# Two transformer-like blocks on one core: the first products after each norm start with high parts, in free PSUM banks

## The chip, the cores and the metric

The kernel runs on one core of one Trainium2 chip. The metric is device time in microseconds (us), the median of three runs. PE is the matmul engine, PEld its weight loads, DVE the vector engine, ACT the scalar engine, POOL the GpSimd engine, and SP the engine that issues nearly all DMAs. Each has its own instruction queue and executes it in order; they meet at semaphores.

## The reference

A sequence of 256 rows of width 1024 (batch 1) passes three layers, all in float32. Each layer is a chain of stages of the same form: normalise the rows, multiply by weights, add to the residual.

```python
# layers 1 and 2; the mixer is attention in the first, an S5 state-space model with GLU in the second
x = x + 0.5 * rmsnorm(swiglu(rmsnorm(x, g[0]), w_in, w_out), g[1])
h = rmsnorm(x, g[2]); x = x + rmsnorm(mixer(h), g[3])
x = x + 0.5 * rmsnorm(swiglu(rmsnorm(x, g[4]), w_in2, w_out2), g[5])
gate = sigmoid(rmsnorm(x, g[6]) @ w_gate)
x = x + rmsnorm(gate * (p[i] @ w_proj), g[7])
# layer 3: as above without the second norm; its mixer is a 128-wide window attention
# beside a gated linear recurrence; rmsnorm at the very end
swiglu(h, w_in, w_out) = (silu(h @ w_in[:, :2816]) * (h @ w_in[:, 2816:])) @ w_out
```

## The kernel before, in words

**Products in two parts.** Every float32 operand is split into a high part (rounded to the matmul format) and a low part (the rest). A product is three matmuls: high by high, high by low, low by high. For the weights, ACT writes the high part (`whi`, L627) from the raw tile that a DMA brought, and DVE the low part (`wlo`, L1103). For the normed rows, PE transposes them into PSUM (L1885), ACT writes `xhi` (L687) from there, and DVE `xlo` (L1208).

**Weights as a ring.** The weights are a stream of 528 half-units of 128x1024. `raw` holds two pairs of half-units, `whi` and `wlo` hold four half-units. A slot of the ring is written again only when PE has reported the half-unit in it as used (`s_used`), and a slot of `raw` is loaded again only when DVE has made the low part of both half-units in it (`s_lo`). At the start of a stage two or all four of its first half-units are ready; where two, ACT splits the next two behind what the change of stage asks of it.

**Settling.** Between two stages the 256 rows are settled in two halves h = 0, 1 of 128 rows: squares (ACT), the reciprocal root (POOL), the residual and the norm (DVE), eight transposes (PE, `transposed`), `xhi` in two quarters kq = 0, 1 (ACT, `evict_hi`), `xlo` in two quarters (DVE, `evict_lo`). `take_turns` writes out the order of these steps over the halves; hooks hang other work behind a step. There are 13 settlings, k = 0 to 12. While it waits, PE runs matmuls on a weight tile whose result nobody reads (`meanwhile`, `fill_in`).

**Stages behind a settling.**
- `ffn(n)`, n = 0 to 5, behind k = 0, 2, 4, 6, 8, 10. Its first half-unit is 24 matmuls of 128x256 (`half_unit`), with both halves of the rows as columns. Column f of the product goes to PSUM bank 4 + f % 3.
- `attention`, behind k = 1: its values product (`values("v0", ...)`) takes four half-units for h = 0 and then for h = 1; the settling of h = 1 (its transposes) comes in between, behind the second half-unit.
- `mixers`, behind k = 9: half-units as in `ffn`, in banks 4 and 5.
- `ple(layer)`, behind k = 3, 7, 11: `project`, a small product of another input, goes to banks 4 to 7 during the settling, and ACT keeps its result in SBUF (`keep`, L741), behind step 7 of the settling. Then comes the gate product into the same banks: `linear` with a head of four half-units through `run`, with the transposes of h = 1 in the middle of it as in `values`.
- The S5 stage and the last store are no part of the change.

**What the first product waits for.** PE waits for `s_xlo` of the whole half or of both halves, that is for the last low part of the rows. In `ffn` bank 4 is also one that the transposes of h = 0 wrote.

Of the kernel before, what the change touches and what calls it, by code (L numbers as in the profile page):

```python
# [8 lines left out]
S = 256  # L9
# [50 lines left out]
SCORE_AT = [j + 2 for j in QK_AT]  # L60

# [65 lines left out]
def program(nc, w, rows, cols, pT, b1c, ssm_s, ssm_b, ssm_c, ssm_cc, oh, idn, eo, x, out, scr):  # L127
# [4 lines left out]
    with ctx:  # L132
# [141 lines left out]
        lv, lp = hf[:, 0, :], hf[:, 1, 0:128]  # L274
# [129 lines left out]
        def sync(sp):  # L404
# [213 lines left out]
        def scalar(a):  # L618
# [79 lines left out]
            def ffn(n):  # L698
                def up(f):
# [8 lines left out]
                    b = 4 + f % 3  # L708
# [20 lines left out]
            def ple(layer):  # L729
# [4 lines left out]

                def keep():
# [11 lines left out]
                settle(k, {3: project, 7: keep})  # L747
# [165 lines left out]
            def mixers():  # L913
# [89 lines left out]
                for j in range(2):  # L1003
                    q.wait_ge(s_used, pair())
                    a.activation(fq[:, 2 * j:2 * j + 2, :], two(4 + n % 2), ACT.Sigmoid).then_inc(m_sf, 1)
# [87 lines left out]
        def vector(v):  # L1093
# [122 lines left out]
            def ffn(n):  # L1216
                def up(f):
# [6 lines left out]
                    v.tensor_tensor(hf[:, f % 2, :], PS[:, 4 + f % 3, S:2 * S], sg[:, f % 2, :], MUL).then_inc(s_hm, 1)  # L1224
# [556 lines left out]
        def tensor(pe):  # L1781
# [13 lines left out]
            def run(parts, base, last, by_half=None, finish=None, step=2, between=None):  # L1795

                for h in range(2):
                    if by_half is not None:
                        q.wait_ge(s_xlo, n_ev(by_half, h))
                    if between and h:  # L1800
                        between()
                    for n, (u, ahi, alo, first, end) in enumerate(parts):
                        if finish and h == 0 and n == 2:
                            finish()
                        hi, lo = weight(u)
                        l_hi, l_lo = ahi[:, 128 * h:128 * h + 128], alo[:, 128 * h:128 * h + 128]
                        for i, (l, r) in enumerate(((l_hi, hi), (l_hi, lo), (l_lo, hi))):
                            for c in range(2):
                                e = mm(PS[:, base + step * h + c, :], l, r[:, 512 * c:512 * c + 512], first and i == 0, end and i == 2)
                        if h:  # L1810
                            e.then_inc(s_used, 1)
                        elif last and n == len(parts) - 1:
                            e.then_inc(s_y, 1)

            def linear(name, acts, base=0, head=1, tail=1, by_half=None, finish=None, ready=None, n_fill=1, step=2, between=None, after=None):
                kts = len(acts)
                v0 = LAST[name] - kts + 1
                for ks in groups(kts, head, tail):
# [8 lines left out]
                    run(parts, base, ks[-1] == kts - 1, by_half if first else None, finish if first else None, step, None if ks[0] else between)  # L1827
                    bg.fill(n_fill)
# [3 lines left out]
            def half_unit(u, o):  # L1832
                hi, lo = (a.rearrange("p (k n) -> p k n", k=8) for a in weight(u))
                for k in range(8):
                    mm(o, hi[:, k, :], xhi[:, k, :], k == 0, False)
                    mm(o, hi[:, k, :], xlo[:, k, :], False, False)
                    e = mm(o, lo[:, k, :], xhi[:, k, :], False, k == 7)
                e.then_inc(s_used, 1)
# [59 lines left out]
            def ffn(n):  # L1898
                k = (0, 2, 4, 6, 8, 10)[n]

                def up(f):
                    b = 4 + f % 3
# [78 lines left out]
            def attention():  # L1981
                def values(name, cols, bank, ns, last, by_half=None):
# [3 lines left out]
                    for h in range(2):  # L1986
                        if by_half is not None:
                            q.wait_ge(s_xlo, n_ev(by_half, h))
                        for n in ns:
                            if by_half is not None and h == 0 and n == 2:  # L1990
# [3 lines left out]
                            for k in range(per):  # L1994
                                kt = per * n + k
                                l_hi, l_lo = (a[:, 128 * h:128 * h + 128] for a in x_acts[kt])
                                for i, (l, r) in enumerate(((l_hi, hi), (l_hi, lo), (l_lo, hi))):
                                    e = mm(PS[:, bank + h, cols], l, r[:, k, :], kt + i == 0, kt == 7 and i == 2)
# [107 lines left out]
            def mixers():  # L2106
# [11 lines left out]
                def pair():  # L2118
                    b = 4 + nb[0] % 2
                    bank_free(nb[0])  # L2120
                    nb[0] += 1
                    half_unit(u0[0], PS[:, b, 0:S])
# [129 lines left out]
                q.wait_ge(s_xlo, n_ev(9, 1))  # L2252
# [242 lines left out]
```

## Time and profile before

| | us |
|---|---|
| median of 3 runs | 1849.22 (1845.55 to 1850.02) |
| profiled execution | 1851.22 |
| its span | 1849.4 |
| PE busy | 1737.1 (94%) |
| DVE busy | 1098.5 (59%) |
| ACT busy | 881.5 (48%) |
| DMA, first queue | 298.66 MB, 45.3% of 16 engines |

The engines' busy shares say that PE is the engine to look at. The mean clock granted to it was 0.972 of full speed. The chain of waits says which engine held the end at each time; the timelines around the eleven stage starts say what PE waits for there.

### The profile page before, as it was taken

Reading aid. Unit: us, or ns where it says so; the run is one execution under the profiler, and the core shown is the slowest. Engines: PE = TensorE matmul, PEld = TensorE weight load, DVE = VectorE, ACT = ScalarE, POOL = GpSimd, SP = SyncE. Lnnn points to the kernel's source line nnn. Section 1 sums busy time; section 2 is a strip of 40 time slices with the busy share of each in tenths; the row PEclk is TensorE's granted clock in tenths of the full one; section 3 lists DMA queues with packets and bytes.
Section 4 is the critical chain, followed back from the end, with each engine's and each line's share of the span. In section 5 each row is a group of like instructions: output and inputs, shape, how many; then the busy total and the mean of one; then the engine's idle time right before and its main releaser. Section 6 shows DMA issues by size and latency. Waiting matters only on the chain.

```text
span 1849.4 us, 28076 instructions
## 1 busy us (share of the span) xinstructions
PE 1737.1 (94%) x11935; PEld 1593.0 (86%) x11935; DVE 1098.5 (59%) x1411; ACT 881.5 (48%) x1370; POOL 166.4 (9%) x192
## 2 busy tenths in 40 slices
PE   7999999899988999998989998999989997999996
PEld 6899789799977998977879997899979887799995
DVE  5455567578765444768565555655556575655554
ACT  5344466443555455452454445544444444444443
POOL 0000001218001012800000000000000000000000
PEclk9999999999999999998999999999999998999998
DMA  6755434445543443531445554465544332455551
GB/s 223 248 175 192 160 140 143 150 183 180 185 171 149 158 165 143 184 136 46 150 153 182 197 179 172 148 215 193 187 151 180 115 115 69 155 196 180 190 184 68
DMA packets 51084, 300.97 MB, mean 163 GB/s; under 512 B 6072, under 2 KB 12688, under 8 KB 17168
## 3 DMA queue, kind: packets, MB, share of 16 engines
q1 hardware_dynamic: 50800, 298.66, 45.3%
q8 instruction: 94, 1.54, 0.3%
q0 software_dynamic: 160, 0.52, 0.1%
q14 instruction: 30, 0.25, 0.0%
HBM read 298.08 MB, written 1.09 MB: 162 GB/s over the span
## 4 chain that ended last, share of the span: by engine, by line
PE 72%; DVE 11%; ACT 9%; DMA 4%; issue 3%; POOL 1%; SPq 0%; DVEq 0%; ACTq 0%; POOLq 0%
PE PS L1786 69%; DVE wlo L1103 4%; DMA raw<-in_w 3%; ACT whi L627 3%; ACT wk L670 1%; PE PS L1789 1%; POOL st L519 1%; PE PS L1885 1%; ACT SC L761 1%; DVE X L1180 1%; DVE SC L1341 1%; DVE xn L1188 1%; ACT SC L848 1%; DVE SC L1496 0%; DVE xlo L1208 0%
## 5 line engine op out<-in xcount | busy, mean ns | idle before, releaser
L1103 DVE TENSOR_TENSOR wlo<-raw,whi 128x1024 fp32r<-128x1024 f32 x528 | 664.5, 1267 | 435.9 <-ACT whi L627 434.3
L1786 PE MATMUL PS<-xhi,whi 128*128 128x256 f32 x2536 | 729.1, 287 | 17.7 <-DVE xlo L1208 9.8
L627 ACT ACTIVATE whi<-raw 128x1024 fp32r<-128x1024 f32 x528 | 550.6, 1054 | 396.1 <-PE PS L1786 230.0
L1786 PE MATMUL PS<-xlo,whi 128*128 128x256 f32 x2536 | 722.7, 285 | 0.0
L1786 PE MATMUL PS<-xhi,wlo 128*128 128x256 f32 x2536 | 722.5, 285 | 0.0
L1786 PEld LDWEIGHTS PS<-xhi,whi 128*128 128x128 f32 x2536 | 492.0, 194 | 26.5 <-DVE xlo L1208 11.4
L1786 PEld LDWEIGHTS PS<-xlo,whi 128*128 128x128 f32 x2536 | 492.3, 194 | 2.1
L1786 PEld LDWEIGHTS PS<-xhi,wlo 128*128 128x128 f32 x2536 | 491.7, 194 | 0.0
L1786 PE MATMUL PS<-whi,hhi 128*128 128x512 f32 x544 | 170.6, 395 | 2.4 <-DVE wlo L1103 2.4
L1786 PE MATMUL PS<-wlo,hhi 128*128 128x512 f32 x544 | 168.6, 391 | 0.0
L1786 PE MATMUL PS<-whi,hlo 128*128 128x512 f32 x544 | 168.3, 390 | 0.0
L709 ACT ACTIVATE wk<-PS 128x256 f32<-128x256 f32 x132 | 50.3, 381 | 156.8 <-PE PS L1786 156.6
L1786 PEld LDWEIGHTS PS<-wlo,hhi 128*128 128x128 f32 x544 | 102.6, 189 | 22.3
L1786 PEld LDWEIGHTS PS<-whi,hlo 128*128 128x128 f32 x544 | 102.4, 188 | 22.1
L1786 PEld LDWEIGHTS PS<-whi,hhi 128*128 128x128 f32 x544 | 98.0, 190 | 19.3 <-DVE wlo L1103 3.0
L1224 DVE TENSOR_TENSOR wk<-PS,wk 128x256 f32<-128x256 f32 x132 | 55.7, 422 | 91.5 <-ACT wk L709 91.3
L512 POOL TENSOR_SCALAR st<-st 128x1 f32<-128x1 f32 x36 | 11.7, 325 | 1072.4 <-ACT wk L670 551.2
L713 ACT ACTIVATE hhi<-wk 128x256 fp32r<-128x256 f32 x132 | 55.2, 418 | 111.0 <-DVE wk L1224 111.0
L1786 PE MATMUL PS<-whi,xhi 128*128 128x512 f32 (+2 forms) x272 | 89.2, 386 | 14.3 <-ACT SC L741 11.8
L1226 DVE TENSOR_TENSOR hlo<-wk,hhi 128x256 fp32r<-128x256 f32 x132 | 60.3, 457 | 63.9 <-ACT hhi L713 63.9
L1786 PE MATMUL PS<-wlo,xhi 128*128 128x512 f32 (+2 forms) x272 | 87.6, 380 | 0.0
L1786 PE MATMUL PS<-whi,xlo 128*128 128x512 f32 (+2 forms) x272 | 87.4, 379 | 0.0
(261 smaller groups left out, 1451.8 us busy)
## 6 DMA issues: line engine op xcount, KB each, us to landing
raw<-in_w SPq DMA_DIRECT2D x264, 1024.0 KB, 4.8
gr<-in_rows SPq DMA_DIRECT2D x23, 512.0 KB, 3.8
SC<-scratch SPq DMA_DIRECT2D x1, 2048.0 KB, 8.4
SC<-scratch SPq DMA_DIRECT2D x2, 1024.0 KB, 8.4
X<-in_x SPq DMA_DIRECT2D x2, 512.0 KB, 4.9
xn<-in_sc SPq DMA_DIRECT2D x2, 512.0 KB, 6.8
out<-xn SPq DMA_DIRECT2D x2, 512.0 KB, 2.7
SC<-in_pT SPq DMA_DIRECT2D x3, 256.0 KB, 4.2
```

Of the source, the lines that this page charges most:

```text
L519: g.tensor_tensor(r, ms, mh[:, 0:max(n, 1)], ALU.pow).then_inc(done, 1)
L627: a.activation(whi[:, u % NSPLIT, :], raw[:, u // 2 % NRAW, u % 2 * HU:u % 2 * HU + HU], ACT.Copy).then_inc(s_hi, 1)
L670: a.activation(wk[:, f], X[:, h, f], ACT.Square, scale=1 / 32, accum_out=ss[:, i:i + 1]).then_inc(s_sq, 1)
L709: a.activation(sg[:, f % 2, :], PS[:, b, 0:S], ACT.Silu).then_inc(s_silu, 1)
L713: a.activation(hhi[:, f % 4, :], hf[:, f % 2, :], ACT.Copy).then_inc(s_hhi, 1)
L761: e = a.activation(pr[:, m, l:z], sc[:, m, l:z], ACT.Exp, bias=n4[:, m, c:c + 1], accum_out=s4[:, m, c:c + 1])
L848: e = a.activation(cst[r, k, :, s, 16 * i:16 * i + 16], o[k][r], ACT.Copy)
L1103: v.tensor_tensor(wlo[:, u % NSPLIT, :], src, hi.bitcast(f32), SUB).then_inc(s_lo, 1)
L1180: v.scalar_tensor_tensor(X[:, h, f], src[:, f], by, X[:, h, f], MUL, ADD).then_inc(s_X, 1)
L1224: v.tensor_tensor(hf[:, f % 2, :], PS[:, 4 + f % 3, S:2 * S], sg[:, f % 2, :], MUL).then_inc(s_hm, 1)
L1226: v.tensor_tensor(hlo[:, f % 4, :], hf[:, f % 2, :], hhi[:, f % 4, :].bitcast(f32), SUB).then_inc(s_hlo, 1)
L1786: return pe.matmul(o, l, r, start=start, stop=stop)
```

## The change

Four edits, with the semaphores kept.

1. **High parts first.** `first_half_unit` takes the place of `half_unit` for the first half-unit of each `ffn` and of `mixers`: for each of eight row tiles it waits for that quarter's `xhi` alone and makes the two products with the high rows; then it waits for `xlo` and makes the eight products with the low rows. In `values("v0")` and in the head of the gate product (`run`), the same is done over the four half-units of each h: sixteen matmuls with high rows, then eight with low rows. `s_used` of a half-unit is counted with its low products.
2. **Other banks.** The first column of `ffn` goes to bank 3 in place of 4, and the first pair of `mixers` to bank 2.
3. **`keep` earlier.** ACT keeps the result of `project` right behind it (hook 3), not behind step 7.
4. **`lv`, `lp` elsewhere.** Two small attention vectors move from the shared `wk` to `prs[1]`, and SP loads them before settling 1, without waiting for the norm.

```diff
+def up_bank(f):
+    return 4 + f % 3 if f else 3
+def pair_bank(n):
+    return 4 + n % 2 if n else 2
...
+            sp.dma_start(lv, ssm_s[2].to_broadcast([128, 256])).then_inc(l_lam, 16)
             settle_rows(1)
-            weights(LAST["v0"])
-            q.wait_ge(s_xn, n_two(1, 1))
-            sp.dma_start(lv, ssm_s[2].to_broadcast([128, 256])).then_inc(l_lam, 16)
...
-                settle(k, {3: project, 7: keep})
+                settle(k, {3: project})
...
 (run)
                 for h in range(2):
-                    if by_half is not None:
-                        q.wait_ge(s_xlo, n_ev(by_half, h))
...
+                    if by_half is not None:
+                        q.wait_ge(s_xhi, n_ev(by_half, h, 0))
+                    for low in (False, True) if by_half is not None else (None,):
+                        if low:
+                            q.wait_ge(s_xlo, n_ev(by_half, h, 0))
...
+            def first_half_unit(u, o, settled):
+                hi, lo = (a.rearrange("p (k n) -> p k n", k=8) for a in weight(u))
+                for k in range(8):
+                    q.wait_ge(s_xhi, n_ev(settled, 1, k // 4))
+                    mm(o, hi[:, k, :], xhi[:, k, :], k == 0, False)
+                    mm(o, lo[:, k, :], xhi[:, k, :], False, False)
+                for k in range(8):
+                    q.wait_ge(s_xlo, n_ev(settled, 1, k // 4))
+                    e = mm(o, hi[:, k, :], xlo[:, k, :], False, k == 7)
+                e.then_inc(s_used, 1)
...
                     if f == 0:
-                        q.wait_ge(s_xlo, n_ev(k, 1))
-                    half_unit(up_at(n, f), PS[:, b, 0:S])
+                        first_half_unit(up_at(n, f), PS[:, b, 0:S], k)
```

On PE, the second gate product (k = 7) from its first matmul on, before. `whi` and `wlo` are its half-units' weights, `idt` rows the transposes of h = 1, and a wait for `s_lo` begins a half-unit:

```order
L1786 MATMUL PS<-whi,xhi 128x512 [waits s_lo,s_xlo,s_prj]
L1786 MATMUL PS<-whi,xhi 128x512
L1786 MATMUL PS<-wlo,xhi 128x512 x2
L1786 MATMUL PS<-whi,xlo 128x512 x2
L1786 MATMUL PS<-whi,xhi 128x512 [waits s_lo]
L1786 MATMUL PS<-whi,xhi 128x512
L1786 MATMUL PS<-wlo,xhi 128x512 x2
L1786 MATMUL PS<-whi,xlo 128x512 x2
L1885 MATMUL PS<-idt,xn 128x128 [waits s_xn]
```

The same stretch after:

```order
L1790 MATMUL PS<-whi,xhi 128x512 [waits s_lo,s_xhi,s_prj]
L1790 MATMUL PS<-whi,xhi 128x512
L1790 MATMUL PS<-wlo,xhi 128x512 x2
L1790 MATMUL PS<-whi,xhi 128x512 [waits s_lo]
L1790 MATMUL PS<-whi,xhi 128x512
L1790 MATMUL PS<-wlo,xhi 128x512 x2
L1910 MATMUL PS<-idt,xn 128x128 [waits s_xn]
```

The low products of the first two half-units no longer stand ahead of the transposes: eight matmuls stand there, not twelve. On PE, the end of the same head (its last two half-units for h = 1, up to the fifth half-unit, which waits for `s_lo`), before:

```order
L1786 MATMUL PS<-whi,xhi 128x512 x2
L1786 MATMUL PS<-wlo,xhi 128x512 x2
L1786 MATMUL PS<-whi,xlo 128x512 x2
L1786 MATMUL PS<-whi,xhi 128x512 x2
L1786 MATMUL PS<-wlo,xhi 128x512 x2
L1786 MATMUL PS<-whi,xlo 128x512 x2
L1786 MATMUL PS<-whi,xhi 128x512 [waits s_lo]
```

and after:

```order
L1790 MATMUL PS<-whi,xhi 128x512 x2
L1790 MATMUL PS<-wlo,xhi 128x512 x2
L1790 MATMUL PS<-whi,xlo 128x512 [waits s_xlo]
L1790 MATMUL PS<-whi,xlo 128x512 x7
L1790 MATMUL PS<-whi,xhi 128x512 [waits s_lo,s_xlo]
```

The eight low products stand at the end in one piece, and with them all four reports of a used half-unit. Before, these came with the 6th, 12th, 18th and 24th matmul of h = 1; now with the 18th, 20th, 22nd and 24th.

On ACT, the same settling, from the weight tile that precedes it, before (L687 writes `xhi`, L670 squares of h = 1, L741 is `keep`):

```order
L627 ACTIVATE whi<-raw 128x1024
L687 ACTIVATE xhi<-PS 128x4x128 [waits s_tr] x2
L670 ACTIVATE wk,st<-X 128x512 [waits s_sq,s_X] x2
L741 ACTIVATE SC<-PS 128x1024 [waits s_y]
L741 ACTIVATE SC<-PS 128x1024 [waits s_used]
```

and after (the lines are L693, L676, L745 there):

```order
L633 ACTIVATE whi<-raw 128x1024
L745 ACTIVATE SC<-PS 128x1024 [waits s_y]
L745 ACTIVATE SC<-PS 128x1024 [waits s_used]
L693 ACTIVATE xhi<-PS 128x4x128 [waits s_tr] x2
L676 ACTIVATE wk,st<-X 128x512 [waits s_sq,s_X] x2
```

The two copies of the projection stand ahead of the high parts and squares, whose order is kept.

## Rows read from the trace of the kernel before

**Rows 1.** Page, chain that ended last: share of the span by engine.
```profile
PE 72%; DVE 11%; ACT 9%; DMA 4%; issue 3%; POOL 1%; SPq 0%; DVEq 0%; ACTq 0%; POOLq 0%
```

**Rows 2.** Waits: engine and line, released by, us in total, times, longest us.
```profile
PE PS L1786 <- DVE xlo L1208: 12.2, 7, 2.5
PE PS L1786 <- ACT SC L741: 11.8, 3, 4.0
```

**Rows 3.** Chain in order of time: start us, us, what; stage starts and matmul rates.
```profile
944.23 184.32 PE PS L1786 x1308
...
1149.61 16.36 PE PS L1786 x72
...
1184.06 185.24 PE PS L1786 x1310
...
1381.30 54.29 PE PS L1786 x406
...
1532.71 2.88 PE PS L1786 x24
...
1608.24 1.98 PE PS L1885 x8
1611.62 194.85 PE PS L1786 x1348
```

**Rows 4.** Timeline, ACT at k = 6, 8, 9: start, us, what, [idle before].
```profile
941.92 1.21 ACT L687 ACTIVATE xhi<-PS 128x512 fp32r<-128x512 f32 x2 [1.65 <-PE PS L1885]
...
1182.08 1.08 ACT L687 ACTIVATE xhi<-PS 128x512 fp32r<-128x512 f32 x2 [2.56 <-PE PS L1885]
...
1378.93 1.26 ACT L687 ACTIVATE xhi<-PS 128x512 fp32r<-128x512 f32 x2 [1.58 <-PE PS L1885]
```

**Rows 5.** Timeline, DVE behind k = 6.
```profile
947.99 3.50 DVE L1103 TENSOR_TENSOR wlo<-raw,whi 128x1024 fp32r<-128x1024 f32 x3 [0.26 <-ACT whi L627]
```

**Rows 6.** Timeline, DVE and PE behind k = 2, DVE behind k = 4.
```profile
361.47 0.61 DVE L1345 TENSOR_SCALAR SC<-SC 128x32 f32<-128x32 f32 x3 [4.95 <-DMA SC<-in_par]
...
365.58 0.50 PE L1786 MATMUL PS<-xhi,whi 128*128 128x256 f32 x1 [1.91 <-DVE wlo L1103]
...
608.19 0.69 DVE L1345 TENSOR_SCALAR xn<-xn 128x1024 f32<-128x1024 f32 x1 [5.69 <-DMA xn<-in_sc]
```

**Rows 7.** Chain: heads of values (k = 1), second and third gate.
```profile
218.64 4.62 PE PS L1786 x12
...
1144.32 4.42 PE PS L1786 x12
...
1811.32 5.34 PE PS L1786 x12
```

**Rows 8.** Timeline, ACT and DVE at the second gate (k = 7).
```profile
1142.34 1.92 ACT L741 ACTIVATE SC<-PS 128x1024 f32<-128x1024 f32 x2
...
1145.24 2.36 DVE L1103 TENSOR_TENSOR wlo<-raw,whi 128x1024 fp32r<-128x1024 f32 x2 [0.33 <-ACT whi L627]
...
1153.82 1.06 ACT L627 ACTIVATE whi<-raw 128x1024 fp32r<-128x1024 f32 x1 [3.52 <-PE PS L1786]
...
1154.91 2.53 DVE L1103 TENSOR_TENSOR wlo<-raw,whi 128x1024 fp32r<-128x1024 f32 x2 [3.78 <-ACT whi L627]
...
1162.30 2.04 ACT L627 ACTIVATE whi<-raw 128x1024 fp32r<-128x1024 f32 x2 [3.41 <-DMA raw<-in_w]
...
1166.00 1.03 ACT L745 ACTIVATE xn<-PS 128x1024 f32<-128x1024 f32 x1 [0.35 <-PE PS L1786]
```

**Rows 9.** Timeline, ACT at the third gate (k = 11).
```profile
1833.94 1.03 ACT L745 ACTIVATE xn<-PS 128x1024 f32<-128x1024 f32 x1 [5.80 <-PE PS L1786]
```

**Rows 10.** Timeline, DVE at the values product (k = 1).
```profile
220.82 2.35 DVE L1103 TENSOR_TENSOR wlo<-raw,whi 128x1024 fp32r<-128x1024 f32 x2
```

**Rows 11.** Windows, PE: us, busy (instructions), granted clock, DMA share, GB/s.
```profile
216.00:218.00 2.00, 0.18 (x2) 1.00 0.50 172
218.00:220.00 2.00, 1.36 (x4) 0.73 0.01 4
```

More of the change, by code:

```diff
@@ L1004, in mixers @@
                     q.wait_ge(s_used, pair())
-                    a.activation(fq[:, 2 * j:2 * j + 2, :], two(4 + n % 2), ACT.Sigmoid).then_inc(m_sf, 1)
+                    a.activation(fq[:, 2 * j:2 * j + 2, :], two(pair_bank(n)), ACT.Sigmoid).then_inc(m_sf, 1)
                     n += 1
@@ L1797, in run @@
                 for h in range(2):
-                    if by_half is not None:
-                        q.wait_ge(s_xlo, n_ev(by_half, h))
                     if between and h:
                         between()
[L1802 to L1813, printed above, removed]
+                    if by_half is not None:
+                        q.wait_ge(s_xhi, n_ev(by_half, h, 0))
@@ new lines, in run @@
+                    for low in (False, True) if by_half is not None else (None,):
+                        if low:
+                            q.wait_ge(s_xlo, n_ev(by_half, h, 0))
+                        for n, (u, ahi, alo, first, end) in enumerate(parts):
+                            if finish and h == 0 and n == 2 and not low:
+                                finish()
+                            hi, lo = weight(u)
+                            l_hi, l_lo = ahi[:, 128 * h:128 * h + 128], alo[:, 128 * h:128 * h + 128]
+                            for i, (l, r) in enumerate(((l_hi, hi), (l_hi, lo), (l_lo, hi))):
+                                if low is None or low == (i == 2):
+                                    for c in range(2):
+                                        e = mm(PS[:, base + step * h + c, :], l, r[:, 512 * c:512 * c + 512], first and i == 0, end and i == 2)
+                            if low is False:
+                                continue
+                            if h:
+                                e.then_inc(s_used, 1)
+                            elif last and n == len(parts) - 1:
+                                e.then_inc(s_y, 1)
@@ L1901, in up @@
                 def up(f):
-                    b = 4 + f % 3
+                    b = up_bank(f)
                     if f >= 3:
@@ L1986, in values @@
                     for h in range(2):
[L1987 to L1990, printed above, removed]
+                        for low, n in [(b, n) for b in (False, True) for n in ns] if by_half is not None else [(None, n) for n in ns]:
+                            if low is not None:
+                                q.wait_ge(s_xlo if low else s_xhi, n_ev(by_half, h, n // 2))
+                            if low is False and h == 0 and n == 2:
                                 transposed(1, 1)
@@ L1997, in values @@
                                 for i, (l, r) in enumerate(((l_hi, hi), (l_hi, lo), (l_lo, hi))):
-                                    e = mm(PS[:, bank + h, cols], l, r[:, k, :], kt + i == 0, kt == 7 and i == 2)
+                                    if low is None or low == (i == 2):
+                                        e = mm(PS[:, bank + h, cols], l, r[:, k, :], kt + i == 0, kt == 7 and i == 2)
+                            if low is False:
+                                continue
                             if h:
```

20 lines of the change are left out of this document (13 added, 7 removed).

## The prediction

> **What bounds the kernel now.** I read the chain of waits first. 72% of the span is PE's [rows 1], so time can come only from PE's own gaps. The view of waits lists them by releaser: the low parts of the rows (L1208) cost PE 12.2 us in seven waits, `keep` (L741) 11.8 us in three [rows 2]. The change aims at these 24.0 us, 1.3% of the time. Then the chain again, at the stage starts, to see what comes behind each: in ffn(3), ffn(4), ffn(5) and `mixers` PE runs on from its first matmul for 184, 185, 195 and 54 us without another releaser [rows 3]. There an earlier start can be kept. Behind k = 2 and k = 4 it is otherwise [rows 6]. The timelines then say when each input is there.
>
> Rates: 24 matmuls of 128x256 take 2.88 us, and 72 of 128x512 take 16.36 us, 0.227 each [rows 3]. At the lower clock twelve of the latter took 4.62, 4.42 and 5.34 us [rows 7] where 12 x 0.227 = 2.73 us would do: a slow spell costs 1.7 to 2.6 us.
>
> **The starts of ffn and mixers.** The new start is the first quarter of `xhi` of h = 1 (half of an L687 row, 0.6 us), with banks 2 and 3 free. 16 matmuls with high rows take 16 x 0.12 = 1.9 us; in that time DVE makes the low parts (at ffn(3) they were there by 944.2, 1.7 us behind `xhi`), so no wait follows.
> - ffn(3): `xhi` at 941.92 + 0.6 = 942.52 [rows 4], start before 944.23 [rows 3]: 1.7 us. But its third half-unit's low part is there only at 947.99 + 1.23 = 949.22, one of the three in 3.50 us [rows 5]; ACT splits no weights there before it has split the projection's input, whose DMA PE's start doesn't move. Before, PE came to it at 944.23 + 2 x 2.88 = 949.99. So 0.7 us is kept, the rest becomes a wait for weights.
> - ffn(4): 1182.68 against 1184.06: 1.35 us [rows 3, 4].
> - mixers: 1379.53 against 1381.30: 1.7 us [rows 3, 4], the PE transposes ending at the same time.
> - ffn(5): the last transpose ends at 1608.24 + 1.98 = 1610.22, start before 1611.62: 1.4 us [rows 3].
> - ffn(1): DVE sits 4.95 us on a parameter DMA until 361.47, and PE then waits 1.91 us for weights until 365.58 [rows 6]. That DMA stands in SP's queue behind loads that go by `s_lo`, and these by the DMA of the projection's input, not by PE. The gain becomes a longer wait: 0.
> - ffn(2): the same with another DMA, 5.69 us until 608.19 [rows 6]: 0.
> - ffn(0): its first matmul needs its first weights' low part, which DVE makes behind all of `xlo`: 0.
> No row shows such a start on high parts. Bounds: nothing (another releaser takes over), and the whole wait, 12.2 us in seven [rows 2]. I take the sum of the single readings, 0.7 + 1.35 + 1.7 + 1.4 = 5.15 us.
>
> **The values product (k = 1).** PE now does eight matmuls as soon as `xhi` is there and is early for the transposes of h = 1. What comes last is the fourth half-unit's low part, at 220.82 + 2.35 = 223.17 [rows 10], which isn't moved. Behind it stand 4 + 8 + 24 = 36 matmuls. Before, 36 matmuls stood behind 218.64 + 4.62 = 223.26 [rows 7] and eight transposes, about 0.9 us (half of the 1.98 us that they took at the lower clock [rows 3]). Gain 0.9 us. The evictions, and the weights behind them, follow the end of this product and shift with it.
>
> **The gates (k = 3, 7, 11).** `keep` goes into idle time of ACT, two copies of 0.96 us [rows 8], while PE transposes; ACT gets to the gate's third and fourth weights up to 1.9 us earlier. DVE does not: it had waited only 0.33 us for them [rows 8], being busy with the norm. So of the 3.9 us wait most goes over to the weights. Second gate: both low parts are there at 1145.24 + 2.36 - 0.33 = 1147.27. h = 1 begins 12 matmuls later; with 0.2 us added, my allowance for the chain's times being those of ends, at 1150.2, where it began at 1149.61 + 2.73 = 1152.3 [rows 3]: 2.1 us ahead. Then comes what the change adds. The first slot of the ring is released with the 18th matmul of h = 1, not the 6th: 1150.2 + 18 x 0.227 + 0.1 = 1154.4 for ACT (0.1 as before: 1152.34 + 6 x 0.227 = 1153.7) instead of 1153.82 [rows 8]. ACT's 1.06 and DVE's 1.23 us follow, and PE, through with its 24 at 1155.7, waits some 1.2 us to 1156.8. Before it came there at 1149.61 + 36 x 0.227 = 1157.8. PE is 1.0 us ahead. But the pair of low parts that lets SP load the next stage's weights ends at 1154.4 + 1.1 + 2.36 = 1157.9 instead of 1154.91 + 2.53 = 1157.44. ACT waits for exactly this load (3.41 us to 1162.30) and has its sigmoid queued behind it, with only 0.35 us to spare [rows 8]. The sigmoid, and the settling behind it, come 0.1 us later, not 1.0 earlier. The first gate is built alike: -0.2 us. The third has no next stage: its sigmoid waits 5.80 us for PE alone [rows 9], so PE's lead counts, and PE's spell was the longest: before 1811.32 + 5.34 + 0.9 + 8.2 = 1825.7 [rows 7], now 1811.32 + 0.92 + 2.36 - 0.33 + 9.5 = 1823.8, taking the distances of the second gate: 1.9 us. Gates together 1.6 us; bounds by rows: the whole 11.8 us of `keep`'s waits [rows 2] as gain, and three slow spells of 1.7 to 2.6 us as loss.
>
> **The clock.** PE's work in these heads falls into pieces: eight matmuls, a gap until the norm of h = 1, transposes, a gap until the third weights, four matmuls, a short gap. At the values product the granted clock was 1.00 of full speed (2.4 GHz) from 216 to 218 us, where PE was busy for 0.18 us, and 0.73 on average from 218 to 220 [rows 11]: it fell to 1.2 GHz after a gap of some 2 us. The early matmuls fill most of that gap; the broken order adds others of 1 to 2 us. I charge one slow spell, 1.7 us, for the values product and the third gate together; at the first two gates ACT's queue hides about 1 us of one.
> The Trainium skill, "TensorE: Matmul & The Clock Gate", section "A second HAM failure mode: psum-queue depth-cycling", says that micro-idles between groups of matmuls are enough to make the clock oscillate although no single gap is long. It speaks against the change; by it each of the four heads pays a spell, which is the slower rival below.
>
> **Rest.** The small attention load feeds two DVE operations that no row of the waits names, and in its new place it has ffn(0) to land: 0. Matmuls and weight loads are as many as before.
>
> **Sum.** 5.15 + 0.9 + 1.6 - 1.7 = 5.95 us. The profiled execution took 1851.22 us (span 1849.4), so a like one would take 1845.3; the median of the runs shown stands 2.0 us below it, so 1849.22 - 5.9 = 1843.3 us, 0.32% faster.
>
> **Rivals.**
> - Both waits go whole and nothing takes their place: 1849.2 - 24.0 = 1825 us. For it: the two rows of waits. Against it: the weights' own timeline at each place. Chance 0.04. Half-way, the starts of ffn(1) and ffn(2) kept and the gates 2 us each: another 3 + 5 us, 1835; chance 0.08.
> - The gain is lost on the way: starts are earlier, but the weights' ring gives it back (DVE or DMA takes over within ffn), or both heads get their slow spell and more. The sum is then 0 to 3 us: 1846 to 1849 us. For it: ffn(1) and ffn(2) do just that. Against it: 184 to 195 us of unbroken PE chain. Chance 0.28. That the change doesn't start PE earlier at all (another releaser at the same time) belongs here.
> - Slower: late release plus chopped work. Each of the four heads pays a slow spell in front, and in each gate the new 1.2 us gap behind h = 1 brings a second: seven spells of 1.7 us, 11.9 us, against the 7.65 us of gains: 1849.2 + 4.3 = 1853.5 us. It decides from five spells on. For it: the clock fell behind a gap at 216 us not longer than the new ones. Against it: in the heads the early matmuls also keep PE busy while it idled. Chance 0.10.
> - My forecast, 1840.5 to 1846 us: chance 0.50.
>
> **From cases to numbers.** A measurement of this kernel tells about 0.3% from no change, 5.5 us: below 1843.7 is faster, above 1854.8 slower. Of the forecast's 0.50 a bit more than half lies below 1843.7, with 0.12 of the first rivals: faster 0.43. The slower rival is centred just inside the bound, so it and unforeseen trouble give slower 0.08. Same 0.49. Range: 1838 to 1850 us leaves out most of the first rivals and the slower one.
>
> **What would show it.** In the profile after: the waits of PE on `xlo` nearly gone, and PE's wait on `keep` gone. PE's first matmul of ffn(3) follows `xhi` at once, with a wait for weights (L1103's counterpart) of about 1 us two half-units later. A new wait for weights of 1.2 us at the fifth half-unit of each gate. In the first two gates ACT's DMA wait ends later relative to the norm, in the third it doesn't matter. The waits behind the parameter DMAs in ffn(1) and ffn(2) grow by 1.4 to 1.6 us. If the ffn(1) and ffn(2) waits stay as they are, or the gates give over 2 us each, the forecast is wrong towards faster; if the granted clock falls more often in the four heads, towards slower.

## The result, and the profile after

The changed kernel took 1844.03 us (median of 12 runs, 1839.70 to 1848.33), the kernel before 1849.17 (12 runs, 1844.84 to 1851.95): ratio 0.9973, 95% interval 0.9962 to 0.9984. That is 5.1 us less; 5.9 had been forecast. In a second comparison the same code came to 0.9948 (0.9936 to 0.9961), 9.2 us less. The two intervals don't overlap.

The waits of PE in the changed kernel (first line by releaser: us in total, times, longest us):

```profile
PE PS L1910 <- DVE xn L1192: 33.8, 18, 7.9
PE PS L1790 <- DVE wlo L1107: 19.8, 13, 4.4
```

L1910 is the transposes (L1885 before), L1790 the matmuls (L1786), L1107 the low parts of the weights (L1103). The two rows of [rows 2], 24.0 us, are gone from the view. In their place stand two others that grew: the wait for the weights' low parts, 19.8 us, was 10.1 us in five waits before, and the transposes' wait for the norm, 33.8 us, was 27.3 us in twelve. Together they took 16.2 of the 24.0 us. So most of the waiting was moved on, not removed.

The chain of the changed kernel (start, us, what) at the stage starts of [rows 3] and the heads of [rows 7]:

```profile
569.21 4.85 DMA raw<-in_w
...
952.57 178.55 PE PS L1790 x1260
...
1148.68 9.38 PE PS L1790 x34
...
1161.63 4.82 DMA raw<-in_w
...
1186.53 185.22 PE PS L1790 x1310
...
1382.66 53.16 PE PS L1790 x406
...
1608.94 194.89 PE PS L1790 x1348
...
1810.48 9.55 PE PS L1790 x34
```

Two things are to be seen. ffn(3) now has a break two half-units behind its start (its chain begins only at 952.57), as forecast; ffn(4), mixers and ffn(5) don't. And in the first two gates the end goes through a load of weights (569.21, 1161.63), in the third through PE alone. 34 matmuls of 128x512 should take 34 x 0.227 = 7.7 us; at 1148.68 and 1810.48 they took 9.4 and 9.6: a slow spell (a stretch at the lower clock) of 1.7 us or more fell on full work.

**Stage lengths.** From the first instruction of one norm of h = 0 (L1192; L1188 before) to that of the next, in us; only ffn(0) is counted from the start of the span. "Starts", "keep" and "heads" are the three parts of the change alone, "old gates" the changed kernel without the new order in its gates; they come below.

| stage | before | changed | changed, again | starts | keep | heads | old gates | again |
|---|---|---|---|---|---|---|---|---|
| ffn(0) | 214.1 | 214.4 | 214.0 | 211.1 | 213.9 | 214.8 | 212.2 | 213.4 |
| attention | 125.8 | 123.6 | 126.3 | 126.5 | 126.2 | 126.4 | 123.7 | 123.6 |
| ffn(1) | 210.7 | 211.2 | 210.1 | 210.8 | 209.0 | 209.1 | 211.3 | 212.2 |
| gate 1 | 37.3 | 37.1 | 36.8 | 37.5 | 35.1 | 40.2 | 35.1 | 35.0 |
| ffn(2) | 230.8 | 232.2 | 230.7 | 230.8 | 231.1 | 233.0 | 231.1 | 230.6 |
| S5 | 117.0 | 120.2 | 117.2 | 117.1 | 117.2 | 117.3 | 117.2 | 120.2 |
| ffn(3) | 202.6 | 202.1 | 201.6 | 201.9 | 202.6 | 202.6 | 202.2 | 202.0 |
| gate 2 | 36.6 | 37.8 | 37.6 | 37.0 | 35.6 | 38.9 | 35.8 | 34.8 |
| ffn(4) | 197.9 | 196.6 | 196.6 | 196.6 | 199.3 | 199.3 | 198.0 | 196.6 |
| mixers | 230.0 | 226.9 | 225.3 | 226.9 | 227.9 | 230.0 | 226.1 | 226.1 |
| ffn(5) | 200.2 | 198.3 | 197.5 | 198.3 | 200.9 | 200.2 | 198.2 | 198.2 |
| gate 3 | 37.2 | 36.9 | 35.6 | 37.2 | 33.1 | 38.7 | 33.1 | 33.0 |
| span | 1849.4 | 1846.5 | 1838.4 | 1840.8 | 1841.0 | 1859.7 | 1833.3 | 1834.8 |

"Lost clock" of a stage is from here on its length times one minus its mean granted clock. The first trace of the changed kernel is a poor witness: its execution was the longest of the twelve, and S5, in which nothing was changed, took 3.2 us more than before. S5 comes in two lengths for one and the same code (last two columns).

### The profile page after: what moved, and what is told of

Its sections match the earlier page's. It is cut to its first block, busy times and chain, and to the rows that moved or that the text cites. A ratio compares the mean times of both kernels' runs of the same rounds, so it can differ in the third digit from the quotient of the medians.

```text
span 1846.5 us, 28080 instructions
## 1 busy us (share of the span) xinstructions
PE 1746.8 (95%) x11935; PEld 1597.7 (87%) x11935; DVE 1094.4 (59%) x1411; ACT 881.6 (48%) x1370; POOL 167.6 (9%) x192
## 4 chain that ended last, share of the span: by engine, by line
PE 78%; DVE 8%; ACT 7%; DMA 3%; issue 2%; POOL 1%; SPq 1%; DVEq 0%; ACTq 0%; POOLq 0%
PE PS L1790 74%; DVE wlo L1107 3%; PE PS L1793 2%; ACT whi L633 2%; ACT wk L676 2%; DMA raw<-in_w 1%; POOL st L525 1%; DVE xn L1192 1%; ACT SC L765 1%; DVE X L1184 1%; PE PS L1910 1%; DMA SC<-in_pT 0%; PE PS L2090 0%; POOL st L518 0%; ACT xn L688 0%
## 5 line engine op out<-in xcount | busy, mean ns | idle before, releaser
L1107 DVE TENSOR_TENSOR wlo<-raw,whi 128x1024 fp32r<-128x1024 f32 x528 | 662.2, 1264 | 443.7 <-ACT whi L633 442.8
L1790 PE MATMUL PS<-xhi,whi 128*128 128x256 f32 x2536 | 727.0, 287 | 12.6 <-DVE wlo L1107 12.0
L1790 PE MATMUL PS<-xhi,wlo 128*128 128x256 f32 x2536 | 720.7, 285 | 0.0
L1790 PE MATMUL PS<-xlo,whi 128*128 128x256 f32 x2536 | 712.5, 284 | 0.0
L1790 PEld LDWEIGHTS PS<-xhi,whi 128*128 128x128 f32 x2536 | 491.5, 194 | 21.1 <-DVE wlo L1107 14.1
L1790 PEld LDWEIGHTS PS<-xhi,wlo 128*128 128x128 f32 x2536 | 491.3, 194 | 0.0
L1790 PEld LDWEIGHTS PS<-xlo,whi 128*128 128x128 f32 x2536 | 486.4, 193 | 2.1
L1790 PE MATMUL PS<-whi,hhi 128*128 128x512 f32 x544 | 170.1, 394 | 2.2 <-DVE wlo L1107 2.2
L1790 PE MATMUL PS<-wlo,hhi 128*128 128x512 f32 x544 | 169.0, 392 | 0.0
L1790 PE MATMUL PS<-whi,hlo 128*128 128x512 f32 x544 | 168.3, 391 | 0.0
L1790 PEld LDWEIGHTS PS<-wlo,hhi 128*128 128x128 f32 x544 | 102.5, 188 | 22.1
L1790 PEld LDWEIGHTS PS<-whi,hlo 128*128 128x128 f32 x544 | 102.6, 189 | 22.1
L1790 PEld LDWEIGHTS PS<-whi,hhi 128*128 128x128 f32 x544 | 97.9, 189 | 18.8 <-DVE wlo L1107 2.4
L1228 DVE TENSOR_TENSOR wk<-PS,wk 128x256 f32<-128x256 f32 x132 | 55.8, 423 | 90.0 <-ACT wk L715 89.8
L1790 PE MATMUL PS<-whi,xhi 128*128 128x512 f32 (+2 forms) x272 | 90.8, 392 | 6.1 <-DVE wlo L1107 5.7
L1790 PE MATMUL PS<-wlo,xhi 128*128 128x512 f32 (+2 forms) x272 | 87.6, 380 | 0.0
L1790 PE MATMUL PS<-whi,xlo 128*128 128x512 f32 (+2 forms) x272 | 79.9, 370 | 0.0
```

The lines of the kernel that those rows point to most:

```text
L1107: v.tensor_tensor(wlo[:, u % NSPLIT, :], src, hi.bitcast(f32), SUB).then_inc(s_lo, 1)
L1228: v.tensor_tensor(hf[:, f % 2, :], PS[:, up_bank(f), S:2 * S], sg[:, f % 2, :], MUL).then_inc(s_hm, 1)
L1790: return pe.matmul(o, l, r, start=start, stop=stop)
```

## Experiments

### The parts of the change, alone

`starts`: of the diff only `first_half_unit`, `up_bank` and `pair_bank`. `keep`: only the copy in `project`. `heads`: only the new `run`, `linear` and `values`. No run has the other banks or the new place of `lv` and `lp` by itself. `old gates`: the changed kernel with this undone:

```
-                    for low in (False, True) if by_half is not None else (None,):
...
-                                if low is None or low == (i == 2):
+                            for c in range(2):
+                                e = mm(...)   # hi*hi, hi*lo, lo*hi of each weight together
```

> The kernel before with one part of the change: high parts first, in banks 3 and 2, for the first half-unit of each ffn and of mixers; heads of gates and values, keep and the small attention load as before. My theory: ffn(3) 0.7, ffn(4) 1.35, mixers 1.7, ffn(5) 1.4 us are kept, ffn(1) and ffn(2) lose theirs to the parameter DMAs: 5.2 us less, ratio 0.997. Rival (the ring of weights takes the gain back within a stage): 0 to 2 us less. In the trace: distance from the norm of k to that of k+1 shorter by those numbers for k = 6, 8, 9, 10.

> The kernel before with one part of the change: keep behind project. Theory L (late release): with the old order the ring's first slot is still released with the sixth matmul of h = 1, and PE does 12 matmuls before the norm of h = 1 is there. h = 1 of the second gate then starts at the weights (1147.3) plus 6 matmuls, some 3.3 us earlier than before, and the sigmoid follows it: 3 us per gate, 9 us in all, ratio 0.995; more than the whole change gave at these three places (0.3 to 0, and 1.2 us lost at the second gate). Rival S (the split gives, keep only clears the way): PE meets the wait for the norm and for weights instead: 0 to 2 us.

> The kernel before with one part of the change: high products first in the heads of the three gates and of the values product; keep at its old place. Theory L: PE starts where it did, h = 1 starts where it did, and the first slot is released 12 matmuls (2.7 us) later; the next stage's weights and the sigmoid behind them come 2.3 us later at the first two gates, PE loses 1.3 us at the third, the values product gains 0.9: 5 us slower, ratio 1.0027. Rival S: the split gains: 0 to 3 us faster.

> The changed kernel with one part taken back: the gates' head has the old order (three products of a half-unit together, waits for the low parts). Theory L: the starts' 5.2, the values product's 0.9 and 3 us per gate: 15 us less than before, ratio 0.992, that is 10 us less than the changed kernel. Rival S: without the split in the gates it is as fast as the changed kernel or slower, ratio 0.997 or more.

Measured against the kernel before (1851.87 us, 16 runs, one chip): `starts` 1842.25 us, ratio 0.9945 (0.9933 to 0.9957); `keep` 1843.96, 0.9955 (0.9943 to 0.9968); `heads` 1858.72, 1.0034 (1.0021 to 1.0047); `old gates` 1837.26, 0.9916 (0.9903 to 0.9928). `keep`, `heads` and `old gates` came out as theory L had it. `starts` gained more than either side expected: 1.3 to 3.1 us at ffn(4), mixers and ffn(5) as it should, but also 2.9 us in ffn(0), 1.7 of it lost clock; that stage takes anything from 211.1 to 214.6 us in traces with this same start. Whether the new start has a part in it isn't shown.

So two good parts and one bad. The sum of the three alone is -9.62 - 7.91 + 6.85 = -10.7 us; the whole change measured -5.1 and -9.2.

Why the heads cost: the second gate. ScalarE (ACT) in the changed kernel, to be held against [rows 8]:

```profile
1139.38 1.92 ACT L745 ACTIVATE SC<-PS 128x1024 f32<-128x1024 f32 x2
...
1158.15 3.91 ACT L633 ACTIVATE whi<-raw 128x1024 fp32r<-128x1024 f32 x4 [9.31 <-PE PS L1790]
1166.47 2.01 ACT L633 ACTIVATE whi<-raw 128x1024 fp32r<-128x1024 f32 x2 [4.42 <-DMA raw<-in_w]
1168.50 1.28 ACT L749 ACT_TABLE_LOAD   x1
1169.80 1.03 ACT L749 ACTIVATE xn<-PS 128x1024 f32<-128x1024 f32 x1
```

and with `keep` alone:

```profile
1149.67 1.06 ACT L627 ACTIVATE whi<-raw 128x1024 fp32r<-128x1024 f32 x1 [3.52 <-PE PS L1784]
...
1158.11 2.09 ACT L627 ACTIVATE whi<-raw 128x1024 fp32r<-128x1024 f32 x2 [3.35 <-DMA raw<-in_w]
1160.21 1.28 ACT L743 ACT_TABLE_LOAD   x1
1161.86 1.03 ACT L743 ACTIVATE xn<-PS 128x1024 f32<-128x1024 f32 x1 [0.36 <-PE PS L1784]
```

The norm begins at 1140.85 and 1135.15. From there the first slot of the ring is free after 17.30 us in the one and 14.52 in the other; 2.8 us later, 12 matmuls of 0.227. Four weights come in one lump (x4) where they were paced one by one. The load that waits for the first pair lands 25.62 against 22.96 us behind the norm, and the sigmoid, no longer waiting for PE but queued behind ACT's weights, starts at 28.95 against 26.71. 2.2 us, for low parts of h = 1 that DVE had ready at 1150.96, before PE came to h = 1 at all (1153.81).

The third gate by windows of 8 us from its norm: length, busy of PE, PEld, DVE, ACT, POOL, and as the last three columns granted clock, DMA share, GB/s. The changed kernel:

```profile
1800.40:1808.40 8.00, 6.37 (x32) 4.85 (x30) 4.42 (x8) 5.90 (x10) 0.84 (x2) 1.00 0.36 133
1808.40:1816.40 8.00, 7.24 (x27) 5.63 (x28) 4.36 (x6) 1.51 (x3) 0.00 (x0) 0.79 0.37 131
```

`keep` alone:

```profile
1798.84:1806.84 8.00, 6.38 (x33) 5.19 (x32) 4.42 (x8) 5.90 (x10) 0.85 (x2) 1.00 0.41 133
1806.84:1814.84 8.00, 7.73 (x39) 6.26 (x38) 4.71 (x7) 2.61 (x5) 0.00 (x0) 1.00 0.40 131
```

39 matmuls against 27 in the second 8 us, at 1.00 against 0.79 of the full clock. With `keep` alone PE fills the time in which h = 1 is normed with twelve matmuls; the new order runs eight, stops, and has the four low products of the first two weights left to do behind the third. The changed kernel's second trace, the same 8 us, parts this from the clock:

```profile
1801.56:1809.56 8.00, 7.23 (x33) 5.49 (x34) 4.36 (x6) 1.51 (x3) 0.00 (x0) 1.00 0.37 131
```

Here the clock stayed at 1.00, and still 33 matmuls stand where `keep` alone has 39; the stage took 35.6 us against 33.1. So 2.5 us is the price of the order itself at this gate, and the slow spell came on top of it in the first trace. The stops, in the timeline of the changed kernel's second gate, PE:

```profile
1146.89 1.32 PE L1910 MATMUL PS<-idt,xn 128*128 128x128 f32 x8 [1.76 <-DVE xn L1192]
1148.68 1.22 PE L1790 MATMUL PS<-whi,xhi 128*128 128x512 f32 x2 [0.48 <-DVE wlo L1107]
1160.61 0.70 PE L1790 MATMUL PS<-whi,xhi 128*128 128x512 f32 x2 [1.20 <-DVE wlo L1107]
```

In front of the transposes, in front of the third weight, and, as forecast, 1.20 us in front of the fifth; the last is 1.20 in all three gates.

### Which half of the rows, the values product, and ffn(1)

Four kernels on another chip (before: 1849.32 us, 12 runs). `second half`: `for low in (False, True) if ... and h == 1`; `first half`: `... and h == 0`; `old values`: `old gates` with the old `values`. `params later`, also from `old gates`:

```
             def scalars():
-                yield
+                for _ in range(5):
+                    yield
                 q.wait_ge(l_par, 64)
...
-                for _ in range(TURN_STEPS):
+                for _ in range(TURN_STEPS - 4):
...   # ScalarE's steps likewise
```

> The changed kernel, but in the gate products only the second half of the rows (h = 1) takes its low parts last; h = 0 has each weight's three products together, as before the change. With both halves in the old order the earlier run had a ratio of 0.9916 to the kernel before. Theory L (the slot of the ring is released late): the first slot goes with the 18th matmul of h = 1 instead of the 6th, 12 x 0.227 = 2.7 us later; in the first two gates ACT waits for the next load about 1 us longer and the sigmoid comes 2.2 us later than in the old order, in the third only PE's 1.2 us wait counts, and ffn(2) behind the first gate gives back 1.3 us more: 6.9 us over the version with the old order, ratio 0.995. Rival C (the broken-up first half and the clock are the price): this version is like the one with the old order, ratio 0.992. Seen by the stage lengths: gate stages 37.3, 37.9, 34.3 us by L, 35.1, 35.8, 33.1 us by C.

> The mirror of the former: only h = 0 takes low parts last, h = 1 is as before the change. Theory L: at the first two gates nothing (h = 1 begins 12.9 to 13.0 us behind the norm's start either way, by the traces of the changed kernel and of the one with the old order); at the third gate the low products of the first two weights stand behind the third weight, 4 x 0.227 = 0.9 us, and a spell at the lower clock falls on full work, 1.7 us: 2.6 us over the version with the old order, ratio 0.993. Rival C: the whole price of the new order, ratio 0.997. Gate stages by L 35.1, 35.8, 35.7 us; by C 37.1, 37.8, 37.0 us.

Measured: `second half` 1839.55 us, ratio 0.9953 (0.9934 to 0.9971), gate stages 36.8, 35.4, 34.5 us; `first half` 1837.88, 0.9943 (0.9931 to 0.9954), 35.0, 35.6, 35.5. The third gate is as theory L had it for both (34.3 and 35.7), and so are the first two of `first half`. At the second gate `second half` cost less than said; its clock never fell there, where the old order lost 1.7 or 3.4 us to it. The three gates together took 106.7 us with the second half's low parts last, 106.2 with the first half's, 102.9 to 104.3 in the six traces of the old order with the early `keep`, and 110.0 to 111.9 in the new. So each half costs 2 to 4 us, by one trace each: the late release is about half of the price, and the broken-up first half the other. The third gate shows it: 33.0 to 33.1 us in the old order, 34.5 with the second half's low parts last and hardly any lost clock (0.2 us), 35.5 with the first half's, but 2.4 us of lost clock in it.

> The version with the gates' old order, and with the first values product in the old order too (low parts with each weight). The attention stage was 2.1 us shorter in each of three traces with the new order of this product and the old gates' or the new ones', and its time at the lower clock fell by half. Theory V (new order of the values product: 0.7 us of order, and one slow spell fewer, 1.4 us): the stage is 125.8 us instead of 123.7 and the ratio to the kernel before 0.9927. Rival (the prediction's 0.9 us, no effect of the clock): 124.6 us, ratio 0.992. Rival 2 (the gain comes from the small attention load's new place, not from the order): the stage stays at 123.7 us, ratio 0.9916.

Measured: 1837.50 us, ratio 0.9941 (0.9929 to 0.9953), above either side's ratio; attention 125.7 us, theory V's length. The load was at its new place here, so that alone (rival 2) doesn't bring the 2.1 us. That it has no part in them isn't shown: the one kernel with the new order and the load at its old place (`heads`) took 126.4. But the next trace, with the new order, has 126.4. In all, the stage took 125.7 to 126.5 us in four traces of the old order, and with the new one 123.6 to 123.7 in seven and 126.3 to 126.4 in three. So the new order doesn't bring 2.1 us as such: the 123.6 or 123.7 comes with 1.7 us of lost clock, all others with 3.4 or 5.1. At 3.4 us the old order took 125.7 and 125.8, the new one 126.3 and 126.4. What is gained is a slow spell fewer, in some executions. Windows of 4 us from the norm, changed kernel, first trace (last three columns: granted clock, DMA share, GB/s):

```profile
214.40:218.40 4.00, 3.08 (x12) 2.33 (x13) 3.49 (x7) 2.45 (x7) 1.51 (x2) 0.74 0.40 135
218.40:222.40 4.00, 2.99 (x13) 1.83 (x11) 3.23 (x6) 3.27 (x6) 0.84 (x2) 0.83 0.07 14
222.40:226.40 4.00, 3.96 (x16) 3.03 (x17) 2.32 (x3) 0.06 (x1) 0.00 (x0) 1.00 0.74 246
...
234.40:238.40 4.00, 3.48 (x29) 3.48 (x30) 3.88 (x4) 2.05 (x3) 0.00 (x0) 1.00 0.30 74
```

and its second:

```profile
214.01:218.01 4.00, 3.03 (x16) 2.27 (x16) 3.49 (x7) 2.48 (x7) 1.51 (x2) 1.00 0.41 135
218.01:222.01 4.00, 1.55 (x10) 0.84 (x8) 3.23 (x6) 3.27 (x6) 0.84 (x2) 0.99 0.08 13
222.01:226.01 4.00, 3.96 (x11) 3.15 (x12) 2.32 (x3) 0.06 (x1) 0.00 (x0) 0.58 0.77 247
...
234.01:238.01 4.00, 2.15 (x10) 2.15 (x11) 3.43 (x4) 3.38 (x4) 0.00 (x0) 0.70 0.06 14
```

The same code, the same gaps. In the first the clock fell early, onto the eight new matmuls, which had time to spare, and did not fall again. In the second it stayed up through them, fell at 222 us on full work and again at 234.

> The version with the gates' old order, and in ffn(1) VectorE takes up the small calculations that need the parameter load four steps later (ScalarE's counterpart too; the four steps are taken from idle steps behind them, so that the rest keeps its place). Theory P (the earlier start of ffn(1) is real and is given back only because VectorE sits on this load until it lands): VectorE makes the weights' low parts and the gated rows in the meantime, PE's waits in the first 20 us of the stage (1.0 us and about 4 us behind wlo) shrink to under 1 us; the stage ffn(1) is 3 to 4.5 us shorter than 211.3 us, ratio to the kernel before 0.9895. Rival (the weights themselves arrive only then, or another releaser takes over): stage 211 us, ratio 0.9916.

Measured: 1832.70 us, ratio 0.9914 (0.9902 to 0.9927), ffn(1) 207.3 us against 211.3. The stage is theory P's; the ratio is the rival's number, but `old gates` ran on another chip, and the comparison on one chip comes below. The waits of PE behind the start of ffn(1), in the changed kernel, in `old gates` and in `params later`:

```profile
352.44 0.39 PE L1790 MATMUL PS<-xhi,whi 128*128 128x256 f32 x1 [0.95 <-DVE wlo L1107]
365.70 0.39 PE L1790 MATMUL PS<-xhi,whi 128*128 128x256 f32 x1 [4.37 <-DVE wlo L1107]
```

```profile
350.47 0.39 PE L1790 MATMUL PS<-xhi,whi 128*128 128x256 f32 x1 [1.04 <-DVE wlo L1107]
...
361.80 0.38 PE L1790 MATMUL PS<-xhi,whi 128*128 128x256 f32 x1 [2.43 <-DVE wlo L1107]
```

```profile
354.58 0.39 PE L1791 MATMUL PS<-xhi,whi 128*128 128x256 f32 x1 [0.78 <-DVE wlo L1107]
```

The second wait is gone. VectorE (DVE) shows why, in `params later` first, then in the changed kernel and in `old gates`:

```profile
353.30 3.49 DVE L1107 TENSOR_TENSOR wlo<-raw,whi 128x1024 fp32r<-128x1024 f32 x3 [0.26 <-ACT whi L633]
356.89 0.42 DVE L1228 TENSOR_TENSOR wk<-PS,wk 128x256 f32<-128x256 f32 x1
```

```profile
351.16 3.50 DVE L1107 TENSOR_TENSOR wlo<-raw,whi 128x1024 fp32r<-128x1024 f32 x3 [0.26 <-ACT whi L633]
361.59 0.61 DVE L1349 TENSOR_SCALAR SC<-SC 128x32 f32<-128x32 f32 x3 [6.94 <-DMA SC<-in_par]
...
362.57 0.42 DVE L1228 TENSOR_TENSOR wk<-PS,wk 128x256 f32<-128x256 f32 x1
```

```profile
357.68 0.61 DVE L1349 TENSOR_SCALAR SC<-SC 128x32 f32<-128x32 f32 x3 [4.99 <-DMA SC<-in_par]
```

The gated rows (L1228) stood queued behind a wait for a small parameter load, whose values no matmul of this stage needs: 6.94 and 4.99 us, 4.95 before [rows 6]. DVE comes to this wait no earlier than before; in the changed kernel it is longer because the load landed later (the wait ends 23.6 us behind the norm, 21.7 in `old gates`, 21.6 before). What PE's earlier start lengthened is PE's own wait: 1.91 us before, 1.04 + 2.43 in `old gates`. The step four places later removes those 2.43 us; of the 4.0 us by which the stage is shorter, 1.7 are lost clock (1.7 against 0.0). Without the step the stage took 208.6 to 212.3 us in twelve traces, with it 207.3 and 207.9.

### The same again side by side, and a filled gap

`filled gap` is the changed kernel with one line:

```
                             if finish and h == 0 and n == 2 and not low:
+                                fill_in(base + 2, parts[0][0], 6)
                                 finish()
```

> The changed kernel unaltered, a second trace of it, beside the next ones on one chip. Its first trace had a span of 1846.5 us, while the median of its runs was 1844.0: S5, whose code is not touched, took 120.2 us there with 17.1 us of lost clock (length times one minus the granted clock), in others 117.0 to 117.3 with 8.5 to 10.1. Theory D (S5 has two outcomes that do not depend on the change): either length may come again; the three gate stages, ffn(2) and mixers keep their lengths to 0.5 us (37.1, 37.8, 36.9, 232.2, 226.9). Rival: S5's 120.2 us belongs to the late low parts and comes again, and the attention's 123.6 us too. Ratio to the kernel before 0.9973 either way.

> The version with the gates' old order again, so that it stands beside the changed kernel on one chip. Theory L: 7 to 9 us under the changed kernel, ratio to the kernel before 0.992 to 0.993, gate stages 35.1, 35.8, 33.1 us. Rival (the earlier difference was one of chips): 2 to 4 us under it, 0.995.

> The version with the gates' old order and the parameter step four steps later, again. Its first run had a median of 1832.7 us, where the same without the later step had 1837.3 on another chip. Theory P: 3 to 4 us under the version with the gates' old order, ratio to the kernel before 0.990; ffn(1) at 207.4 us against 211.3. Rival: the attention stage, 126.4 us in its first trace, takes the gain back, so that the two are within 1 us.

> The changed kernel, and in each gate's first half six matmuls more (128x512, high weights by themselves, into a bank that is written anew later; their result is not used) between the eight early ones and the transposes of h = 1, where PE stood idle for 1.6 to 1.8 us. Theory S (this gap is what lets the clock fall to the lower level on the second half of the work at the gates): the granted clock stays at 1.00 through the head, at the third gate 1.7 us are won (36.9 to 35.2 us), at the first two PE is 1.7 us earlier and all of it reaches ACT's load and the sigmoid (37.1 and 37.8 to 35.4 and 36.1): 5 us, ratio 0.9945. Rival (the two gaps of 0.5 us around the transposes suffice, or the clock falls on another occasion): no stage gains over 0.3 us, ratio 0.997. Rival 2 (the fillers delay the transposes): stages 0.3 us longer.

On one chip, before 1850.05 us (12 runs): the changed kernel 1840.89, 0.9948 (0.9936 to 0.9961); `old gates` 1837.76, 0.9929 (0.9914 to 0.9943); `params later` 1834.51, 0.9909 (0.9894 to 0.9924), the fastest version, 15.5 us under the kernel before and 6.4 under the changed one; `filled gap` 1845.13, 0.9973 (0.9959 to 0.9987). `params later` is 3.3 us under `old gates`, as theory P said (3 to 4), and not within 1 us of it, though the two intervals overlap.

Theory D holds for S5 and the attention, which both came out at their other length. ffn(2) and mixers didn't keep theirs to 0.5 us as I had said (1.6 us less each); of the gates the first two stayed within 0.3 us. The third came out at 35.6 us with the granted clock at 1.00 throughout, 36.9 with a spell. `old gates` has the ratio of theory L, but is only 3.1 us under the changed kernel, not 7 to 9: the rival's number. Yet its gate stages are 7.1 us shorter in the same pair of traces; S5 (+3.0) and ffn(1) (+2.0) go the other way, the attention (-2.7) the same. How much of the gates' 7 us reaches the median stays open between 3 and 7.

`filled gap`: theory S fell. The clock did stay up at the second gate (no lost clock; 1.7 us at the first, 0.8 at the third), PE reached the release there 1.1 us earlier than in the changed kernel's first trace, and nothing came of it:

```profile
1152.49 3.91 ACT L633 ACTIVATE whi<-raw 128x1024 fp32r<-128x1024 f32 x4 [8.17 <-PE PS L1790]
1162.15 2.01 ACT L633 ACTIVATE whi<-raw 128x1024 fp32r<-128x1024 f32 x2 [5.76 <-DMA raw<-in_w]
```

ACT's wait for the load grew from 4.42 to 5.76 us. The load took some 6.2 us behind the pair of low parts, against 4.7 to 4.9 at this gate in the thirteen other traces; why it was slower isn't shown. Gate stages 38.0, 38.1, 35.6, the third no shorter than without the filler. Why the median is 4 us above the unfilled kernel's isn't settled either.

## Why the prediction was right, point by point

The time, the range and the direction held, in part by luck. The terms held unevenly:

- **Starts of ffn.** ffn(3): 0.7 forecast, 0.5 and 1.0 measured, with the forecast wait for weights (0.87 us at 952.57). ffn(4): 1.35 forecast, 1.34 measured. ffn(5): 1.4 forecast; 2.0 and 2.7 measured, with 1.7 and 3.4 us less lost clock than before. The wait of 1.41 us for the low parts is gone, so the start is as forecast and the rest goes with the spells. ffn(0) and ffn(2): 0 forecast, nothing beyond what the same code varies by. ffn(1): 0 forecast, and the stage gained nothing. The mechanism was right: PE's gain became a longer wait for weights behind the same parameter DMA, as `params later` shows by taking it away.
- **mixers.** 1.7 forecast, 3.1 and 4.8 measured. The start itself gave what was forecast. With `keep` alone, which doesn't touch this start, and in the changed kernel's second trace no spell fell in the first 70 us of the stage; there ACT splits the ninth weight behind the norm at

```profile
1399.06 1.06 ACT L627 ACTIVATE whi<-raw 128x1024 fp32r<-128x1024 f32 x1 [0.91 <-PE PS L1784]
```

```profile
1398.11 1.06 ACT L633 ACTIVATE whi<-raw 128x1024 fp32r<-128x1024 f32 x1 [0.91 <-PE PS L1790]
```

that is 29.0 and 27.3 us behind the norms at 1370.05 and 1370.81: 1.7 us. The rest is where and how often a spell falls: `keep` has the stage 2.1 us shorter than before by that alone.

- **Values product.** 0.9 us forecast; -0.5 or 2.2 measured, by where the spell falls. At equal lost clock the 0.9 doesn't show. The step that failed is the clock.
- **The clock.** -1.7 us forecast, one spell more. In the attention and the three gates together the lost clock was 15.1 us before and 6.8 in both traces of the changed kernel, 17.8 in `heads`. So the sign was wrong for the whole change. How much of this reached the time isn't shown; the gates as a whole didn't get shorter by it.
- **Gates.** 1.6 us in sum forecast, -0.7 and +1.1 measured. The failed step is "h = 1 begins 12 matmuls later ... at 1150.2": its first matmul started at 1153.81, 13.0 us behind the norm instead of 1150.2 - 1138.26 = 11.9, since a spell fell on the sixteen matmuls ahead of it (5.1 us for them, against 4.0 at the third gate of the second trace, at full clock). The sigmoid came 28.95 us behind the norm, where it was 1166.00 - 1138.26 = 27.74 before [rows 8]: 1.2 us later instead of 0.1. The wait of 1.20 us and ACT's 4.42 us for the load, with the sigmoid behind it, were right. The first gate's sigmoid came 0.2 and 0.5 us earlier behind the norm, for 0.2 later. The third gate gave 0.3 us with a spell and 1.6 without, for 1.9.
- **What the sum hid.** I priced keep and the new order together, at 1.6 us. Alone, `keep` shortens the gates by 2.1, 1.0 and 4.2 us, and the new order takes 6 to 8 us of it back by the traces. The forecast was right because a gain and a loss, neither priced, nearly cancel: that is luck. The wait behind `keep` was [rows 2]'s 11.8 us in PE's idle time. With `keep` alone PE still waits in front of the gates (1.46, 1.91 and 1.62 us) until DVE has the low parts of h = 0. The view names no releaser for it, but at the second gate DVE's row ends at 1139.09, and PE starts at 1139.19:

```profile
1137.81 1.28 DVE L1206 TENSOR_TENSOR xlo<-PS,xhi 128x512 fp32r<-128x512 f32 x2
```

```profile
1139.19 1.19 PE L1784 MATMUL PS<-whi,xhi 128*128 128x512 f32 x2 [1.91 <-issue]
```

The new order takes this wait away, and PE runs into the next: 1.76 us for the norm of h = 1, which isn't moved. At the second gate PE then comes to the third weight 2.2 us earlier than with `keep` alone (7.8 against 10.1 us behind the norm), but sixteen matmuls stand behind it in place of twelve, some of them at the lower clock, and h = 1 begins no earlier: 13.0 us behind the norm against 12.9. So the second edit gains nothing once the first is made. That question I did not ask.

- **The slower rival.** Its mechanism, late release and chopped work, is real: `heads` alone is 0.34% slower. Its count of seven spells was not: over the whole span the lost clock of the kernel before is 52.4 us, of the changed kernel 50.5 and 36.8, of `heads` 58.2. The Trainium skill ("TensorE: Matmul & The Clock Gate", section "A second HAM failure mode: psum-queue depth-cycling") holds micro-idles between groups of matmuls, where they are frequent enough, to make the clock oscillate. `heads` agrees weakly, with 5.8 us more lost clock, 2.7 of them in its four heads' stages; the changed kernel, whose heads are broken up in the same way, doesn't.

## What to carry to other kernels

Price the edits of a change one by one and in order: when one removes a wait, ask again what the others are for. Putting a product's late operand last pays at the start of a stage where PE then runs on (0.5 to 1.7 us each here). Inside a ring of weights it also holds the slots back, and it costs where the operand wasn't late (h = 1) or where another wait follows at once (h = 0). And before an engine is made to start earlier, look at what stands in another engine's queue behind the next load: moving one wait for a small load four steps back won 3.3 us in the medians, about what the earlier starts of ffn(3), ffn(4) and ffn(5) were forecast to bring together (3.45 us).

## What the runs showed of the hardware

- Unchanged code comes in several lengths. S5 took 116.9 to 117.3 us, 118.8 or 120.2, with 8.5 to 10.1, 14.9 or 17.1 us of lost clock. A stage's lost clock goes mostly in steps of 1.7 us (0.0, 1.7, 3.4 or 5.1 in the attention and most of ffn), and the same gaps cost a step in one execution and none in the next. One pair of traces can't tell a 2 us effect of an edit from this; the attention stage took fourteen.
- A lower clock costs nothing where the engine has time to spare. In the attention stage the cheapest outcome was the one in which the clock fell first (123.6 us, the fall on eight matmuls in front of the transposes; 126.3 with it on full work).
